# Expert slots numbered by expert and rank, a row gather for every pair of experts, 18 ring slots, and a down projection that leaves its two halves for combine

## The chip, the cores and the metric

The kernel runs on one core of one Trainium2 chip. The metric is the device time of one execution in microseconds; the median of three runs is given, and one more execution was taken with the profiler.

## The reference

Two transformer-like blocks over 256 tokens of width 1024, batch 1, in fp32. The first has a projection, sparse attention, retention and a merge. The second has a state-space branch, latent attention, a cross attention over a memory, and then the mixture of experts that this change is about. All of it up to the router is the same in both kernels. Cut to what matters:

```python
def hierarchical_moe(h, w_rg, b_rg, w_re, b_re, w_gate, w_up, w_down):
...
    g_prob = jax.nn.softmax(g_logits, axis=-1)
    g_sel = jnp.argmax(g_logits, axis=-1)
...
    top_v, top_i = lax.top_k(e_in, TOP_K)
    w_top = jax.nn.softmax(top_v, axis=-1) * g_w
    expert_id = g_sel[:, None] * EXPERTS_PER_GROUP + top_i
    combine = jnp.sum(jax.nn.one_hot(expert_id, N_EXPERTS, dtype=jnp.float32) * w_top[..., None], axis=1).astype(t.dtype)
    hg = jnp.einsum('td,edf->tef', t, w_gate)
    hu = jnp.einsum('td,edf->tef', t, w_up)
    act = jax.nn.silu(hg) * hu * combine[:, :, None]
    y = jnp.einsum('tef,efd->td', act, w_down)
...
h = h + hierarchical_moe(rms_norm_2(h, norm_moe[i]), ...)
...
return rms_norm_2(h, norm_final)
```

A token belongs to one of 4 groups of 8 experts, and goes through two experts of its group: silu(x W_gate) * (x W_up), times W_down (256 x 1024), times a weight; the two results are added to the residual h. The 256 tokens give 512 (token, expert) entries, called slots.

## The kernel before

All dense projections run from a stream of 1 MB weight units: SyncE loads a unit into `raw` (3 slots), ScalarE makes `whi` and POOL `wlo` of it (3 slots each), and TensorE multiplies in three fp32r passes. The last units are those of `xo` (output of the cross attention) and `rt` (the router, unit 111). After them comes the part that changes.

The expert weights (three parts of an expert: gate/up rows 0 to 511, gate/up rows 512 to 1023, down; each 1 MB) are loaded by SyncE (L507 for "e" entries, L515 for "o" entries) into a ring of `NRING` = 13 slots of 8 KB per partition. Experts are worked on in pairs. `pair_plan` gives 24 pairs in a fixed order: 16 pairs "e" of two experts each, and 8 pairs "o" that take what an expert has over `TS` = 32 tokens. The loads of an "o" pair have a condition and are skipped on the chip when there is nothing over; the matmuls of an "o" pair run in any case. Before the first load of an "o" pair SyncE waits for `over_ready` (L510), the table of these further tiles, that VectorE makes in `overflow()`. An entry of the ring waits until the unit that held its slot has been used (`first_used`, `gu_full` or `y_full`). The first four slots lie in memory that is free early, the others only after the router's matmuls (`weights_used` = NU).

Slots are packed: the 512 entries, sorted by expert, stand in 512 columns. VectorE makes `pick` (256 tokens x 512 slots, ones where a token fills a slot), and TensorE gathers all rows at once (L2345, L2346: the normed rows split in two fp32r parts, 8 blocks of 128 features with 512 moving columns), ScalarE copies the result to `xs`. Then, for each pair, POOL cuts the window of 32 columns of each expert out of `xs` (L547, `window`) and the slots' weights out of `wrow` (L554, `weights`).

For each pair j TensorE does: `gate_up(j)` (L2393: 32 fp32 matmuls with 32 stationary columns, in four column groups of the array), `act_transposed` (L2378), `down` (L2409: 8 fp32 matmuls of 512 columns into four column groups of one bank, accumulated over the two halves k of the hidden width), and `combine` (L2419: 4 fp32r matmuls with `sT`, the one-hot map from slots to tokens, into the banks ps4 to ps7 that accumulate over all pairs). In this order: `gate_up(j)` with the transposes of j-1 within it, `combine(j-2)`, `down(j-1)`. ScalarE does `silu` (L903) and `y_hi` (L909, L910), VectorE `gate` (L1695), `act_copy` (L1703, which multiplies with the slots' weights), `owners` (L1711, L1713: makes `sT`) and `y_lo` (L1720: the rest of the split of y in fp32r parts, four instructions on 32 partitions). At the end VectorE adds the residual (L1782), ScalarE squares (L922), VectorE scales (L1790), and four stores go out.

Of the kernel before, what the change touches and what calls it, by code (L numbers as in the profile page):

```python
# [22 lines left out]
UW = 2048  # L23
# [11 lines left out]
NRING = 13  # L35
# [6 lines left out]
for _n, _w in (("ident", 128), ("tri", 128), ("stri", 128), ("ones", 128), ("cmpmask", 30), ("cos", 16), ("sin", 16),  # L42
               ("invf", 16), ("iota", 32), ("rcos", 128), ("rsin", 128), ("negmask", 128), ("slot", 1)):
    CONST[_n] = (sum(w for _, w in CONST.values()), _w)
# [72 lines left out]
def pair_plan():  # L117

    pairs = []
    for n in range(NEXP // 2):
        pairs.append(("e", n))
        if n % 2 == 0 and n or n == 3:
            pairs.append(("o", len(pairs) - n - 1))
    return pairs


def ring_plan(npair):


    ring = []
    for j in range(npair + 1):
        if j < npair:
            ring += [(j, part, u) for part in range(2) for u in range(2)]
        if j:
            ring += [(j - 1, 2, u) for u in range(2)]
    return ring


def bank_plan(units):
# [58 lines left out]
    G += [("xg", k) for k in range(8)]  # L200
# [24 lines left out]
    W += [("rtt", 0), ("cn", 0), ("ds", 0), ("wr", 0), ("pT", 0), ("od", 0)]  # L225
# [12 lines left out]
def program(nc, x_d, mem_d, pos_d, cst_d, sml_d, dec_d, npost_d, nfin_d, w_d, ew_d, out_d):  # L238
# [9 lines left out]
    NT = len(PAIRS)  # L248
    RING = ring_plan(NT)
    ENTRY = {u: n for n, u in enumerate(RING)}  # L250
    ctx = ExitStack()
    with ctx:
# [128 lines left out]
        xnh = at("xnh", A + 8 * KB, [P, TT, DM], f32r)  # L381
        xnl = at("xnl", A + 16 * KB, [P, TT, DM], f32r)
        pick = at("pick", A + 24 * KB, [P, TT, NSLOT], f32r)
        ramp = at("ramp", A + 28 * KB, [P, NSLOT])
        a = A + 30 * KB
        oh = at("oh", a, [P, 2, TT, 32])
        msum = at("msum", a + 512, [P, TT, 32])
        prod = at("prod", a + 768, [P, 2, TT, 32])
        cnt = at("cnt", a + 1280, [32, P])
        offn = at("offn", a + 1792, [P, 2, 32])  # L390
        row = at("row", a + 2048, [P, 8, 32])
        over = at("over", a + 3072, [P, 8, NOVER])
        posf = at("posf", a + 3584, [P, 4])
        start = at("start", a + 3616, [P, NEXP + NOVER], i32)
        mine = at("mine", a + 3840, [P, NPAIR])
        overi = at("overi", a + 4064, [P, 2, NOVER], i32)
        rtl = at("rtl", A + 38 * KB, [P, 8, TT * 36])
        lgt = at("lgt", A + 38 * KB + 2304, [36, S])
        flt = at("flt", A + 42240, [32, P])
        xw = at("xw", A + 42 * KB, [P, 2, 8, 2 * TS])  # L400
        sg = at("sg", A + 46 * KB, [P, 2, 256])

        yhl = at("yhl", A + 8 * KB, [P, 2, 2, 512], f32r)
        ac = at("ac", A + 28 * KB, [2 * TS, 2, 256])
        tally = at("tally", A, [P, 2, NEXP])
        match = at("match", A + 512, [P, NOVER, NEXP])
        mval = at("mval", A + 512 + 2 * KB, [P, NOVER, NEXP])
        vals = at("vals", A + 512 + 4 * KB, [P, 4, NEXP])
        aT = at("aT", A + 22 * KB, [P, 2, 4 * TS])
        nfin = at("nfin", A + 24 * KB, [P, DM])  # L410
        xs = at("xs", base + 9 * UW * 4, [P, 8, NSLOT])
        a = base + 9 * UW * 4 + 16 * KB
        posT = at("posT", a, [P, 2 * S])
        sT = at("sT", a + 2 * KB, [P, 2, S], f32r)
        wrow = at("wrow", a + 4 * KB, [P, NSLOT])
        wx = at("wx", a + 6 * KB, [P, 2, 2 * TS])
        wpick = at("wpick", a + 8 * KB, [P, TT, NSLOT])
        diag = at("diag", a + 12 * KB, [P, 4, P])
        wtmp = at("wtmp", a + 14 * KB, [P, NSLOT])
        ring = [at(f"ring{i}", A + (48 + 8 * i) * KB if i < 4 else base + (i - 4) * UW * 4, [P, UW])[:, :] for i in range(NRING)]  # L420

# [56 lines left out]
        def _(sp):  # L478
# [40 lines left out]
        def _(pool):  # L519
# [14 lines left out]
            nc.gpsimd.iota(ramp[:, :], [[1, NSLOT]], base=0, channel_multiplier=0, allow_small_or_imprecise_dtypes=True).then_inc(sem("ramp_ready"), 1)  # L534

            starts = {}

            def window(j):
                kind, k = PAIRS[j]
                if kind == "o":  # L540
                    pool.wait_ge(sem("over_ready"), 1)
                k = 2 * k + NEXP * (kind == "o")
                starts[j] = [pool.value_load(start[0:1, k + u:k + u + 1], min_val=0, max_val=NSLOT - TS) for u in range(2)]
                if j >= 2:
                    pool.wait_ge(sem("gu_full"), j - 1)
                for u in range(2):
                    ins = pool.tensor_copy(xw[:, j % 2, :, TS * u:TS * u + TS], xs[:, :, bass.ds(starts[j][u], TS)])  # L547
                ins.then_inc(sem("rows_ready"), 1)

            def weights(j):  # L550
                if j >= 2:
                    pool.wait_ge(sem("aT_ready"), j - 1)
                for u, first in enumerate(starts.pop(j)):
# [1978 lines left out]
```

## Time and profile before

| | before |
|---|---|
| median of three runs | 1198.32 us (1196.86 to 1198.56) |
| the profiled execution | 1198.53 us |
| its span, first to last instruction | 1196.7 us |
| PE busy | 1023.9 us (86%) |
| POOL busy | 612.6 us (51%) |
| DVE busy | 619.5 us (52%) |
| ACT busy | 426.6 us (36%) |
| mean granted TensorE clock | 0.931 |
| DMA in the last quarter of the span | up to 421 GB/s |

The span is what the trace shows; the execution's own time has 1.83 us more. PE is TensorE's matmuls, PEld its weight loads, DVE VectorE, ACT ScalarE, SPq the queue of SyncE. Matmuls overlap in the records, so the spacing of their starts says more than their durations. An fp32 matmul is two instructions in the trace, an fp32r one or a transpose is one.

### The profile page before, as it was taken

What the parts mean: (1) busy time and instruction counts of PE and PEld (TensorE: products, weight loads), DVE (VectorE), ACT (ScalarE), POOL (GpSimd) and SP (SyncE); (2) the same over time, 40 slices, a digit from 0 to 9 for tenths busy, and PEclk for the clock granted to TensorE, in tenths of its full rate; (3) what the DMA queues carried; (4) which work ended last, traced back from release to release, by engine and by line L of the source; (5) the groups of instructions that cost most, each with busy time, mean ns of one, the idle gap of its engine ahead of it and who ended that gap; (6) DMA issues with size and microseconds to landing.
All of it is one profiled execution on the core that took longest, in us unless ns stands there. A gap on an engine that the chain in (4) does not pass through costs nothing.

```text
span 1196.7 us, 19506 instructions
## 1 busy us (share of the span) xinstructions
PE 1023.9 (86%) x7452; PEld 840.0 (70%) x7452; DVE 619.5 (52%) x1343; ACT 426.6 (36%) x637; POOL 612.6 (51%) x549
## 2 busy tenths in 40 slices
PE   5897899987957979999999999999985879787773
PEld 4786788987946869999977789898964534333331
DVE  6303246368545665554159986842116656444445
ACT  4543333332224545554434344344432311111111
POOL 5997814456748676664765349888540011110100
PEclk9999898999987889999999999999996879999996
DMA  6554522333334344332433226554434589999990
GB/s 251 172 204 160 192 71 71 100 131 123 140 107 141 139 143 141 139 121 96 145 137 106 97 81 211 176 172 170 155 138 189 234 340 413 420 421 420 420 398 36
DMA packets 31907, 224.90 MB, mean 188 GB/s; under 512 B 3664, under 2 KB 3664, under 8 KB 5072
## 3 DMA queue, kind: packets, MB, share of 16 engines
q1 hardware_dynamic: 30672, 220.07, 48.9%
q10 hardware_dynamic: 1152, 3.67, 0.9%
q8 instruction: 59, 0.97, 0.3%
q14 instruction: 24, 0.20, 0.0%
HBM read 273.01 MB, written 1.05 MB: 229 GB/s over the span
## 4 chain that ended last, share of the span: by engine, by line
POOL 44%; issue 31%; DMA 12%; PE 9%; DVE 3%; SPq 0%; ACT 0%; POOLq 0%; DVEq 0%
POOL wlo L524 44%; DMA ring<-in_experts 12%; PE ps L2393 3%; PE ps L2409 1%; PE ps L2419 1%; DVE yhl L1720 1%; PE ps L2345 0%; PE ps L2346 0%; PE ps L1807 0%; PE ps L1809 0%; PE ps L1808 0%; PE ps L2378 0%; POOLq L527 0%; DVE x L1782 0%; SPq L507 0%
## 5 line engine op out<-in xcount | busy, mean ns | idle before, releaser
L524 POOL TENSOR_TENSOR wlo<-raw,whi 128x512 fp32r<-128x512 f32 x448 | 583.6, 1336 | 308.4 <-ACT whi L580 307.9
L1857 PE MATMUL ps<-xhi,whi 128*128 128x256 f32 x960 | 283.6, 295 | 10.5 <-DVE xlo L1210 4.1
L1858 PE MATMUL ps<-xhi,wlo 128*128 128x256 f32 x960 | 277.7, 289 | 0.0
L1859 PE MATMUL ps<-xlo,whi 128*128 128x256 f32 x960 | 277.4, 289 | 0.0
L580 ACT ACTIVATE whi<-raw 128x2048 fp32r<-128x2048 f32 x112 | 214.0, 1914 | 147.0 <-PE ps L1859 75.2
L1857 PEld LDWEIGHTS ps<-xhi,whi 128*128 128x128 f32 x960 | 191.0, 199 | 14.7 <-issue 7.1
L1858 PEld LDWEIGHTS ps<-xhi,wlo 128*128 128x128 f32 x960 | 190.6, 199 | 1.0 <-issue 0.7
L1859 PEld LDWEIGHTS ps<-xlo,whi 128*128 128x128 f32 x960 | 190.4, 198 | 0.0
L2393 PE MATMUL ps<-ring,xw 128*32 128x256 f32 x1536 | 103.6, 407 | 33.0 <-DMA ring<-in_experts 32.3
L1807 PE MATMUL ps<-whi,xhi 128*128 128x512 f32 (+3 forms) x298 | 117.8, 395 | 13.1 <-POOL wlo L524 11.1
L547 POOL COPY xw<-xs 128x256 f32 x48 | 20.4, 452 | 209.9 <-PE ps L2393 162.7
L1808 PE MATMUL ps<-wlo,xhi 128*128 128x512 f32 (+3 forms) x298 | 114.9, 386 | 0.0
L1809 PE MATMUL ps<-whi,xlo 128*128 128x512 f32 (+3 forms) x298 | 114.6, 385 | 0.0
L2393 PEld LDWEIGHTS ps<-ring,xw 128*32 128x32 f32 x1536 | 52.7, 114 | 77.3 <-issue 58.3
L1720 DVE TENSOR_TENSOR yhl<-ps,yhl 32x512 fp32r<-32x512 f32 x96 | 65.9, 687 | 75.9 <-ACT yhl L910 74.8
L1807 PEld LDWEIGHTS ps<-whi,xhi 128*128 128x128 f32 x298 | 57.6, 193 | 26.6 <-POOL wlo L524 10.5
L1808 PEld LDWEIGHTS ps<-wlo,xhi 128*128 128x128 f32 x298 | 57.6, 193 | 10.7 <-issue 1.0
L1809 PEld LDWEIGHTS ps<-whi,xlo 128*128 128x128 f32 x298 | 57.6, 193 | 10.3
L1150 DVE TENSOR_REDUCE stat<-ps 128x1 f32<-128x128 f32 (+1 forms) x36 | 11.0, 306 | 90.0 <-PE ps L1918 69.7
L2409 PE MATMUL ps<-ring,aT 128*32 128x512 f32 x384 | 49.0, 629 | 9.6 <-issue 6.8
L903 ACT ACTIVATE sg<-ps 128x256 f32<-128x256 f32 x24 | 9.2, 384 | 119.2 <-PE ps L2393 119.2
L658 ACT ACTIVATE pr<-ps,stat 128x128 f32<-128x128 f32 x64 | 26.2, 415 | 55.8 <-DVE stat L1151 55.8
(465 smaller groups left out, 1496.0 us busy)
## 6 DMA issues: line engine op xcount, KB each, us to landing
ring<-in_experts SPq DMA_DIRECT2D x144, 1024.0 KB
raw<-in_weights SPq DMA_DIRECT2D x112, 1024.0 KB, 4.9
x<-in_x SPq DMA_DIRECT2D x2, 512.0 KB, 4.5
memt<-in_mem ACTq DMA_DIRECT2D x1, 1024.0 KB, 6.0
out<-xn ACTq DMA_DIRECT2D x4, 256.0 KB, 2.5
decay<-in_decay ACTq DMA_DIRECT2D x1, 512.0 KB, 4.1
npost<-in_norm_post ACTq DMA_DIRECT2D x1, 512.0 KB, 5.4
nfin<-in_norm_final ACTq DMA_DIRECT2D x1, 512.0 KB, 8.1
```

The costliest lines, as they stand in the source:

```text
L524: ins = pool.tensor_tensor(wlo[:, j, c], raw[:, j, c], whi[:, j, c].bitcast(f32), ALU.subtract)
L580: act.activation(whi[:, n % NSPL, :], raw[:, n % NRAW, :], ACT.Copy).then_inc(hi_ready, 1)
L658: ins = act.activation(p_buf[:, c], pj((S_, u))[:, c], ACT.Exp, bias=stat[:, NMAX + k + t:NMAX + k + t + 1], accum_out=stat[:, sums + k + ...
L1720: ins = v.tensor_tensor(yhl[other, j % 2, b, :], ps[3][own, :], yhl[own, j % 2, b, :].bitcast(f32), ALU.subtract)
L1807: mm(out, lh, rh, start=first, stop=False, skip_group_check=skip)
L1808: mm(out, lh, rl, start=False, stop=False, skip_group_check=skip)
L1809: return mm(out, ll, rh, start=False, stop=last, skip_group_check=skip)
L1857: mm(o_, wh[:, k, cc], hi[:, k0 + r0 + k, :], start=first, stop=False, skip_group_check=True)
L1858: mm(o_, wl[:, k, cc], hi[:, k0 + r0 + k, :], start=False, stop=False, skip_group_check=True)
L1859: ins = mm(o_, wh[:, k, cc], lo[:, k0 + r0 + k, :], start=False, stop=last, skip_group_check=True)
L2393: ins = mm(ps[j % 2][q:q + TS, 0:256], xw[:, j % 2, 4 * part + k, TS * u:TS * u + TS], wt[u][:, k, 256 * h:256 * h + 256], start=first, st ...
L2409: ins = mm(ps[3][q:q + TS, :], aT[:, j % 2, 2 * TS * k + TS * u:2 * TS * k + TS * u + TS], wt[u][:, k, 512 * h:512 * h + 512], start=k == ...
```

## The change

- Slots are numbered by expert and rank: expert e owns slots 32e to 32e + 31, and entries beyond rank 31 get slots of the further tiles. `rank` comes from one product with the mask `before` over `msum`.
- The gather is done for each pair, from the unsplit fp32 `xn`: `gather(j)` on TensorE (16 matmuls with a 128x128 stationary part of `xn` and 64 moving columns of `pick`), then `rows_out` on VectorE writes `xw`. `pick` is made for each pair by `pick_rows` from `codes` (VectorE). The gather of 512 columns, `xs`, `wrow`, `wpick` and POOL's copies go; POOL makes only an iota in this stage.
- The slots' weights come from one more small product (`slot_weights`, `weights_of_slots`) as one column per pair in `wslot`, and are put on in `y_hi` and `y_lo`.
- The ring has 18 slots, in places that come free at three times: four as before; entries 4 to 6 in the `raw` slots, entries 7 to 13 once `weights_used` is NU - 1, entries from 14 on once it is NU. Entries stand in the order of the pairs.
- The "o" pairs stand at other places in the order; the first is the fifth pair (before, the fourth).
- TensorE's order for a pair: `gate_up(j)`, `gather(j+1)`, `act_transposed(j)`, `combine(j-1)`, `down(j)`. With j = 0, `code_rows` and `weights_of_slots` come in between, with j = 1 `residual_in`.
- `down` writes one bank per half h of the output columns, and its column groups hold (expert u, half k of the hidden width); the sum over k happens in `combine`, which takes eight matmuls (h, token tile t, part). The y parts are made in two instructions each, of 128 partitions.
- The residual enters ps4 to ps7 through a product with the identity; the last norm's squares and scaling read these banks.

```diff
-NRING = 13
+NRING = 18
@@ pair_plan
-        if n % 2 == 0 and n or n == 3:
+        if n in (3, 4, 5, 7, 9, 11, 13, 14):
@@ ring_plan
+    return [(j, part, u) for j in range(npair) for part in range(3) for u in range(2)]
@@ SyncE
-                if n == 4:
+                if 4 <= n < 7:
+                    sp.wait_ge(lo_ready, NU - 6 + n)
+                if n == 7:
+                    sp.wait_ge(weights_used, NU - 1)
+                if n == 14:
                     sp.wait_ge(weights_used, NU)
@@ ScalarE
+            def y_hi(j):
                 act.wait_ge(sem("y_full"), j + 1)
+                w = wslot[:, PLACE[j]:PLACE[j] + 1]
+                for h in range(2):
+                    act.activation(yhl[:, h, 0, :], ps[2 + h][:, :], ACT.Copy, scale=w).then_inc(sem("y_hi_ready"), 1)
+            act.wait_ge(sem("combined"), NT)
             for t in range(TT):
+                for h in range(2):
+                    k = STAT["f"] + 2 * t + h
+                    act.activation(xn[:, t, 512 * h:512 * h + 512], ps[4 + 2 * t + h][:, :], ACT.Square, accum_out=stat[:, k:k + 1]).then_inc(sem("squares_f"), 1)
@@ VectorE
+            def pick_rows(j, at_):
+                do(v.tensor_tensor(hit[:, :, :], C("iota").unsqueeze(1).to_broadcast([P, 4, 2 * TS]), ALL4(at_, 2 * TS), ALU.is_equal))
+                sync()
+                v.tensor_tensor(pick[:, j % 2, :, :], hit[:, 0:2, :], hit[:, 2:4, :], ALU.add).then_inc(sem("pick_ready"), 1)
+            def rows_out(j):
+                dve.wait_ge(sem("gathered"), j + 1)
+                v.tensor_tensor(xw[:, j % 2, :, :], ps[1][:, :].rearrange("p (k s) -> p k s", k=8),
+                                D("g_moe").unsqueeze(2).to_broadcast([P, 8, 2 * TS]), ALU.mult).then_inc(sem("rows_ready"), 1)
             def owners(j):
+                do(v.tensor_scalar(own[:, :], posT[:, :], -2.0 * TS * PLACE[j], C("slot"), ALU.add, ALU.is_equal))
+                sync()
+                v.tensor_tensor(sT[:, j % 2, :], own[:, 0:S], own[:, S:2 * S], ALU.add).then_inc(sem("owners_ready"), 1)
             def y_lo(j):
+                for h in range(2):
+                    dve.wait_ge(sem("y_hi_ready"), 2 * j + h + 1)
+                    v.scalar_tensor_tensor(yhl[:, h, 1, :], ps[2 + h][:, :], wslot[:, PLACE[j]:PLACE[j] + 1],
+                                           yhl[:, h, 0, :].bitcast(f32), ALU.mult, ALU.subtract).then_inc(sem("y_lo_ready"), 1)
             for j in range(NT):
                 if j:
                     y_lo(j - 1)
                 gate(j)
+                if j + 1 < NT:
+                    rows_out(j + 1)
                 act_copy(j)
                 if j == 0:
+                    slot_weights()
+                    wait_full(dve, ("ws", 0))
+                    release(v.tensor_copy(wslot[:, :], pj(("ws", 0))[:, 0:NPAIR]), ("ws", 0))
+                    wait_done(dve, ("ws", 0))
+                    further()
+                    wait_done(dve, ("pT", 0))
+                owners(j)
+                if j + 2 < NT:
+                    pick_rows(j + 2, codes[:, PLACE[j + 2], :])
@@ TensorE
+            def gather(j):
+                pe.wait_ge(sem("pick_ready"), j + 1)
+                for k in range(8):
+                    for t in range(TT):
+                        ins = mm(ps[1][:, 2 * TS * k:2 * TS * k + 2 * TS], xn[:, t, k * P:k * P + P], pick[:, j % 2, t, :], start=t == 0, stop=t == 1)
+                ins.then_inc(sem("gathered"), 1)
             def down(j):
+                for h in range(2):
+                    for u in range(2):
+                        for k in range(2):
+                            q = TS * (2 * u + k)
+                            ins = mm(ps[2 + h][q:q + TS, :], aT[:, 2 * TS * k + TS * u:2 * TS * k + TS * u + TS], wt[u][:, k, 512 * h:512 * h + 512], start=True, stop=True)
+            def combine(j):
+                pe.wait_ge(sem("owners_ready"), j + 1)
+                for h in range(2):
+                    pe.wait_ge(sem("y_lo_ready"), 2 * j + h + 1)
+                    for t in range(TT):
+                        for part in range(2):
+                            ins = mm(ps[4 + 2 * t + h][:, :], sT[:, j % 2, t * P:t * P + P], yhl[:, h, part, :], start=False, stop=part == 1 and j == NT - 1)
+            for j in range(NT):
+                gate_up(j)
+                if j == 0:
+                    code_rows()
+                if j + 1 < NT:
+                    gather(j + 1)
+                act_transposed(j)
+                if j == 0:
+                    weights_of_slots()
+                if j == 1:
+                    residual_in()
+                if j:
+                    combine(j - 1)
+                down(j)
             combine(NT - 1)
```

## Rows read from the trace of the kernel before

**Rows 1.** Chain of waits, 860 to 1197 us, shares by line.
```profile
by line: DMA ring<-in_experts 41.6%; PE ps L2393 11.1%; issue 9.0%; PE ps L2409 4.9%; POOL wlo L524 3.7%; PE ps L2419 3.3%; DVE yhl L1720 2.5%; PE ps L2345 1.6%; PE ps L2346 1.4%; PE ps L1807 1.3%; PE ps L1809 1.3%; PE ps L1808 1.3%; PE ps 
```
**Rows 2.** Windows: length, busy us of each engine (instructions), clock, DMA share, GB/s.
```profile
900.00:910.00 10.00, 5.81 (x30) 4.47 (x29) 6.45 (x21) 5.47 (x12) 0.56 (x1) 0.75 0.00 0
...
920.00:930.00 10.00, 6.88 (x23) 5.94 (x23) 6.38 (x27) 0.69 (x1) 0.00 (x0) 0.50 1.01 425
...
950.00:960.00 10.00, 4.19 (x66) 2.05 (x54) 9.40 (x27) 0.97 (x2) 1.04 (x4) 0.81 0.18 75
960.00:970.00 10.00, 9.43 (x90) 3.85 (x86) 5.07 (x11) 1.47 (x3) 1.24 (x4) 0.68 0.73 284
...
1040.00:1060.00 20.00, 16.11 (x164) 7.47 (x168) 7.52 (x15) 2.74 (x6) 2.35 (x8) 0.83 1.01 421
```
**Rows 3.** DMA queues, 860 to 1197 us: packets, MB, share.
```profile
q1 hardware_dynamic: 13972, 101.72, 73.1%
```
**Rows 4.** Waits of SyncE's queue, 860 to 1197 us: total, times, longest.
```profile
SPq L510 <- DVE mine L1661: 12.7, 1, 12.7
```
**Rows 5.** Timeline of TensorE near 1000 us: start, length, line, tiles, count.
```profile
999.15 1.20 PE L2419 MATMUL ps<-yhl,sT 128*128 128x512 f32 x4
1000.33 1.92 PE L2409 MATMUL ps<-ring,aT 128*32 128x512 f32 x16
1002.04 2.80 PE L2393 MATMUL ps<-ring,xw 128*32 128x256 f32 x48
1004.78 0.34 PE L2378 MATMUL ps<-cst,ac 64*128 64x64 f32 x2
```
**Rows 6.** Timeline from the last dense unit to the first pairs.
```profile
899.92 0.40 PE L1809 MATMUL ps<-whi,xlo 128*128 128x512 f32 x1
...
904.95 1.57 PEld L1892 LDWEIGHTS ps<-cst,xn 128*128 128x128 f32 x8 [3.65 <-DVE xn L976]
...
919.08 1.06 PE L2327 MATMUL ps<-cst,msum 128*32 128x128 f32 x4 [5.74 <-DVE msum L1623]
...
923.44 0.29 DVE L1628 TENSOR_TENSOR prod<-oh,ps 128x128 f32<-128x128 f32 x1 [2.98 <-PE ps L2337]
...
936.61 1.88 PE L2352 MATMUL ps<-wpick,cst 128*128 128x512 f32 x4
...
938.32 1.05 PE L2356 MATMUL ps<-diag,cst 128*128 128x128 f32 x8
...
940.59 6.25 PE L2393 MATMUL ps<-ring,xw 128*32 128x256 f32 x112 [0.65 <-ACT posT L598]
...
947.88 0.68 DVE L1744 TENSOR_TENSOR mval<-cst,tally 128x512 f32<-128x512 f32 x1
```
**Rows 7.** Groups by line, 880 to 1197 us: busy, mean ns, idle before.
```profile
L2393 PE MATMUL ps<-ring,xw 128*32 128x256 f32 x1536 | 103.6, 407 | 33.0 <-DMA ring<-in_experts 32.3 <-ACT posT L598 0.7
L1720 DVE TENSOR_TENSOR yhl<-ps,yhl 32x512 fp32r<-32x512 f32 x96 | 65.9, 687 | 75.9 <-ACT yhl L910 74.8
...
L1695 DVE TENSOR_TENSOR ac<-sg,ps 32x256 f32<-32x256 f32 x48 | 20.1, 418 | 25.2 <-ACT sg L903 24.5
...
L909 ACT ACTIVATE yhl<-ps 128x512 fp32r<-128x512 f32 x24 | 14.3, 597 | 84.0 <-PE ps L2409 84.0
```
**Rows 8.** Timeline of TensorE in the scan stage, near 614 us.
```profile
614.00 1.89 PE L2226 MATMUL ps<-xtok,segM 128*128 128x64 f32 x16
615.73 0.65 PE L2209 MATMUL ps<-segR,cst 128*128 128x512 f32 x1
```
**Rows 9.** Timeline of TensorE in a dense projection, near 100 us.
```profile
100.29 0.28 PE L1857 MATMUL ps<-xhi,whi 128*128 128x256 f32 x1
100.41 0.28 PE L1858 MATMUL ps<-xhi,wlo 128*128 128x256 f32 x1
```
**Rows 10.** Timeline of the tail, after the last combine.
```profile
1184.87 2.48 DVE L1782 TENSOR_TENSOR x<-ps,x 128x512 f32<-128x512 f32 x4 [2.23 <-PE ps L2419]
...
1192.33 1.41 DVE L1790 SCALAR_TENSOR_TENSOR xn<-x,stat,nfin 128x512 f32<-128x512 f32 x2
```

More of the change, by code:

```diff
@@ L391, in program @@
[L391 to L420, printed above, removed]
+        a = [A + 8 * KB]
@@ new lines, in program @@
+        msum = small("msum", [P, TT, NEXP])
+        prod = small("prod", [P, 2, TT, NEXP])
+        cnt = small("cnt", [NEXP, P])
+        flt = small("flt", [NEXP, P])
+        tally = small("tally", [P, 2, NEXP])
+        match = at("match", a[0], [P, NOVER, NEXP])
+        mval = at("mval", a[0] + 2 * KB, [P, NOVER, NEXP])
+        nfin = small("nfin", [P, DM])
+        over = small("over", [P, 2, NOVER])
+        overi = small("overi", [P, 2, NOVER], i32)
+        choice = small("choice", [P, 8, 4])
@@ new lines, in program @@
+        posT = small("posT", [P, 2 * S])
+        xw = small("xw", [P, 2, 8, 2 * TS])
+        ac = small("ac", [2 * TS, 256])
+        aT = small("aT", [P, 4 * TS])
+        slots = [A + (48 + 8 * i) * KB for i in range(4)]
+        slots += [base + 8 * KB * i for i in (1, 2, 0)]
+        slots += [base + 8 * KB * i for i in (4, 7, 5, 8)] + [base + 80 * KB, base + 96 * KB, A + 40 * KB]
+        slots += [base + 8 * KB * i for i in (3, 6)] + [base + 72 * KB, base + 88 * KB]
+        ring = [at(f"ring{i}", o, [P, UW])[:, :] for i, o in enumerate(slots)]
@@ L533, in _ @@
             pool.wait_ge(sem("mn_ready"), 2)
[L534 to L553, printed above, removed]
-                    ins = pool.tensor_copy(wx[:, j % 2, TS * u:TS * u + TS], wrow[:, bass.ds(first, TS)])
-                ins.then_inc(sem("wx_ready"), 1)
-            pool.wait_ge(sem("start_ready"), 1)
-            for k in range(4, 8):
-                wait_done(pool, ("xg", k))
-            window(0)
-            window(1)
-            wait_done(pool, ("wr", 0))
-            for j in range(NT):
-                weights(j)
-                if j + 2 < NT:
-                    window(j + 2)
+            nc.gpsimd.iota(islot[:, :], [[TS, 2], [0, 2], [1, TS]], base=0, channel_multiplier=0, allow_small_or_imprecise_dtypes=True).then_inc(sem("islot_ready"), 1)
         @block.scalar
@@ new lines, in _ @@
+            do(v.tensor_scalar(flt[:, :], cnt[:, :], float(TS), None, ALU.is_gt))
+            for q in range(2, NSTEP + 1):
+                sync()
+                ins = v.scalar_tensor_tensor(flt[:, :], cnt[:, :], float(TS * q), flt[:, :], ALU.is_gt, ALU.add)
+                if q < NSTEP:
+                    do(ins)
+            ins.then_inc(sem("more_ready"), 1)
+            rows_out(0)
+            wait_full(dve, ("od", 0))
+            release(v.tensor_copy(tally[:, :, :], pj(("od", 0))[:, 0:64].rearrange("p (a e) -> p a e", a=2)), ("od", 0))
@@ L2362, in _, with code_rows, weights_of_slots @@
             end(ins, ("od", 0))
-            od_bank = JOBS[("od", 0)][0]
-            for b in range(8):
-                if b != od_bank:
-                    pe.wait_ge(bank_done[b], TOTAL[b])
+            def code_rows():
+                pe.wait_ge(sem("diag_ready"), 1)
+                begin(("pT", 0))
+                for i in range(4):
+                    ins = mm(pj(("pT", 0))[:, i * P:i * P + P], ones, diag[:, i, :], start=i == 0, stop=i == 3, skip_group_check=True)
+                end(ins, ("pT", 0))
+            def weights_of_slots():
+                pe.wait_ge(sem("which_ready"), 2)
+                begin(("ws", 0))
+                for i in range(4):
+                    ins = mm(pj(("ws", 0))[:, 0:NPAIR], which_slot[:, i, :], which_pair[:, i, :], start=i == 0, stop=i == 3)
+                end(ins, ("ws", 0))
             def unit(j, part, u):
@@ L2392, in gate_up @@
                                 q = TS * (2 * u + h)
[L2393 to L2395 removed]
+                                ins = mm(ps[0][q:q + TS, 0:256], xw[:, j % 2, 4 * part + k, TS * u:TS * u + TS], wt[u][:, k, 256 * h:256 * h + 256], start=first, stop=last)
                     if part == 0:
```

329 lines of the change are left out of this document (116 added, 213 removed).

## Prediction

> **What bounds the kernel now.** I read the page first, then the chain of waits, the windows, the DMA view and the timeline, all for the last 337 us, because the diff touches only what follows the last dense projection. In that stretch the chain is held by the expert weights: 41.6% is DMA into the ring, against 11.1% for the gate/up matmuls [rows 1]. The windows show why: from 960 to 1160 us the 16 DMA engines stand at a share of 1.01 and about 421 GB/s while TensorE is busy 16 of 20 us [rows 2]. A unit is 1,048,576 bytes, so it takes 1.0486 / 0.421 = 2.49 us. The queue moved 101.72 MB [rows 3], which is 97 units: one raw unit and the 96 of the sixteen "e" pairs. So no expert had more than 32 tokens, the eight "o" pairs load nothing, and TensorE still does their matmuls. DMA lies idle twice: around 900 to 910 us (0 GB/s), and around 950 to 960 us (75 GB/s), where the queue stands 12.7 us at the overflow table [rows 2, 4].
>
> The reader should see that there are two clocks in this stage. DMA needs 96 x 2.49 = 239 us. TensorE needs 24 pairs times what one pair costs it, and now that is less. Start to start in the timeline at full clock: 48 gate/up instructions 2.74 us, four combine instructions 1.18, sixteen down instructions 1.71; the two transposes have 0.33 with their fill, some 0.27 to the next start [rows 5]. All 64 gate/up instructions are thus 2.74 x 64/48 = 3.65 us, and a pair is 3.65 + 0.27 + 1.18 + 1.71 = 6.8 us, 163 us for 24. It ends second.
>
> **The change, part by part.**
>
> *Ring of 18 slots, loads from earlier.* Units 4 to 6 go into raw slots, units 7 to 13 once the last xo unit is used (its last matmul starts at 899.92 [rows 6]), and 14 to 17 after the router. That uses the idle DMA window: 14 x 2.49 = 35 us of loading, of which nine units ran at this place before. All 18 are there by about 928. The other 78 need 78 x 2.49 = 194 us and could end near 1126, where they end near 1165 now. The first overflow pair also comes later in the list (unit 24), and its table needs fewer operations. By itself this part is worth some 30 to 40 us, if DMA stays the bound.
>
> *The gather, new in every pair.* Instead of one gather of 512 columns (32 fp32r instructions) and cheap POOL copies, each pair does 16 fp32 matmuls with a 128x128 stationary part of xn and 64 moving columns. An fp32 matmul is two instructions in this trace (768 gate/up calls are 1536 records [rows 7]), so 32 per pair. The trace has this very form: 16 instructions of 128x64 fp32, each with fresh 128x128 weights, run from 614.00 to the next group at 615.73, 1.73 us or 108 ns each [rows 8]; it has four such groups at full clock, all of 1.73. The gather is 3.46 us. The lower bound is that the weights hide behind the moving side, as for the 256-column fp32r instructions, which start every 120 ns, 13 more than their 107 ns of columns [rows 9]: 64 fp32 columns at the 0.43 us per 512 of four instructions in 1.71 us [rows 6] are 53 ns, 1.7 to 2.1 us in all. The upper bound is the cold 200 ns per weight load [rows 6], 6.4 us. I take 3.46, the row of the same form. The Trainium skill, "TensorE: Matmul & The Clock Gate", section "LDWEIGHTS (loading the stationary operand)", prices a load by columns over 1.2 GHz, 107 ns for 128, and the row agrees (108).
>
> *Down and combine.* Down keeps 8 calls, 16 instructions and four column groups, only with k in the group instead of the accumulation: 1.71 us as before. Combine goes from four instructions to eight. The form (fp32r, 512 columns) has 213 ns of columns plus some 14; four more are 0.91 us: 1.18 + 0.91 = 2.09.
>
> *Sum for one pair:* 3.65 + 3.46 + 0.27 + 2.09 + 1.71 = 11.18 us. The lower bound, 53 ns per gather instruction, is 9.4; a few tenths for hand-overs give 11.8.
>
> *Is it back to back?* VectorE per pair: y_lo 2 x 0.69, gate 2 x 0.42 [rows 7], act_copy 0.29 as another 128x128 from PSUM [rows 6], rows_out and owners at some 0.7 each for 512 columns, pick_rows about 0.65; under 6 us. silu and gate (0.4 + 0.84) lie under the 3.46 of the next gather; rows_out and act_copy (1.0 after the gather) under transposes and combine (2.36); y_hi and y_lo (2.6 after down) under gate/up. So no wait is left inside a pair. POOL leaves the stage, which costs nothing. Loads: the longest run of e, e, o needs 2 x 14.9 = 30 us of DMA against 33.5 of TensorE, so the ring is full when asked. TensorE takes over as the bound.
>
> *Front.* The masks' matmuls start at 919.08 [rows 6]. Then the two ds matmuls (1.0 us cold), prod and reduce 0.29 each, three small ones and pick_rows (together 1.3): gather(0) starts near 922.1. TensorE is at half clock there (0.50, its 1.2 GHz [rows 2]), so 32 x 0.215 = 6.9 us, the cold load and a little; ready 929.0, rows_out 0.8, gate/up(0) at 929.9. It starts at 940.59 now [rows 6], so 10.7 us earlier. The whole hi/lo gather, wpick, wrow and most of the tile table go from this path.
>
> *First two pairs.* Gate/up(0) to 933.5; code_rows 1.0 [rows 6]; gather(1) to 938.0; transposes 938.3. Then TensorE waits for VectorE: rows_out, act_copy and the 13 operations of slot_weights (4.1), so 942.4; ws 1.0, down(0) 945.1, gate/up(1) 948.8. VectorE meanwhile does further() (seven operations, six at 0.69 [rows 6], 4.4), owners and pick_rows(2): gather(2) starts at 949.7, not 948.8. Then 3.46, transposes 0.27, the residual through the identity (8 instructions x 0.43 = 3.44), combine 2.09, down 1.71: 960.7. The 4 us of idle before ws can drop the clock, as an idle TensorE did at 950 to 970 (0.81, then 0.68 [rows 2]). Ten microseconds at 0.68 lose 3.2; I add 2.3, for the idle here is shorter. Pair 1 ends at 963.
>
> *Rest.* 22 pairs x 11.18 less the one gather that the last lacks (3.46) is 242.5: down(23) ends at 1205.5. Behind it two y_hi (0.6 [rows 7] and 0.55), the second y_lo 0.69, half a combine 1.15 and hand-overs: 3.1, so 1208.6. The tail is 11.83 now, 1184.87 to 1196.7 [rows 10]. The four adds (2.48) go; four squares of 512 with accumulator reads replace two of 1024, and the first now waits for both halves. By the chain: 1.4 of squares, 1.9 of root, 1.4 of scaling, 1.9 and 1.4 again, 3.0 of store: 11.0. Span 1219.6.
>
> The profiled execution took 1198.53 us for a span of 1196.7, so 1.83 lie outside; 1221.4. It was 0.21 above the median of 1198.32, so I say 1221.
>
> **The rivals.**
>
> A. *The gather's weight loads hide* (ends on the other side). The place is the 32 instructions of each gather. For it: the 120 ns rows [rows 9]. Against: the groups of the same form show 108 ns [rows 8]. At 57 ns a gather is 1.8 us, 1.65 less in 23 of them, 38 us: 1183. It decides from the point where a gather takes less than 2.45 us (77 ns per instruction): then the 23 us lost are given back. Chance 0.09.
>
> B. *The loads hide in part.* Half way between 57 and 108 ns is 82: 0.83 less in each of 23 gathers, 19 us: 1202. No row of this form shows it. Chance 0.06, half of it within 0.2%. The Trainium skill bears on it: the same page, section "Back-to-back issue gap", gives about 81 ns for a sustained stream of loads and matmuls of 128 columns, and one of the 64-column fp32 instructions streams as long as such a matmul.
>
> C. *DMA stays the bound.* The chain would again show ring loads; the end would be 1126 plus the last pairs and tail, near 1155, or 1160. That needs pairs under 9 us on TensorE, so A and more. Chance 0.02.
>
> D. *Hand-overs or the clock cost more.* If each pair waits 1 us (down on act_copy, or gather on pick_rows), 22 us: 1243. If TensorE ran half of the first 30 us cold besides, 1250. For it: TensorE works through five hand-overs a pair, and I cost them at nothing; against: each of them has over 1 us of cover by the durations above. Chance 0.14.
>
> My forecast itself: 0.69.
>
> **How the numbers follow.** Faster or slower by 0.2% (2.4 us) is what a measurement can tell. Faster: A, C and a tail of B, 0.12. Same: 0.03. Slower: 0.85. The likeliest case has its own range: the pair between 10.7 and 11.7, 22 times, and 4 us either way in the front, 1208 to 1235. The range takes in B and most of D: 1201 to 1241.
>
> **What would show it.** Right: the chain of waits names the gather, gate/up, down and combine lines and hardly DMA; TensorE over 95% busy and its clock at full (2.4 GHz) from 965 on; gather groups of 32 instructions 3.4 to 3.6 us apart from the next group; pairs 11.2 us apart, also the "o" pairs; DMA gaps inside each cycle, last ring load 20 us and more before the last combine; gate/up(0) near 930. Wrong: gather groups near 2 us (A); DMA share still 1.01 after 1000 (C); idle before down, or before the gather, ended by VectorE (D); a last load that comes after TensorE has asked for it.

## The result, and the profile after

| | before | after |
|---|---|---|
| median, us (range) | 1198.44 (1196.86 to 1200.69, 4 runs) | 1224.18 (1223.84 to 1226.33, 4 runs) |
| profiled execution, us | 1198.53 | 1223.84 |
| its span, us | 1196.7 | 1222.1 |
| granted TensorE clock, mean | 0.931 | 0.954 |

After over before is 1.0222, with a 95% interval from 1.0201 to 1.0244. The changed kernel is slower, at a higher mean clock.

The chain that ended last, from 860 us on, answers to [rows 1]; the line gives shares by engine and source line:

```profile
by line: PE ps L2290 25.5%; PE ps L2346 23.5%; PE ps L2376 13.6%; PE ps L2359 12.8%; issue 5.0%; POOL wlo L528 2.4%; PE ps L2333 1.7%; PE ps L1766 1.2%; PE ps L1768 1.2%; PE ps L1767 1.1%; PE ps L2368 1.0%; DVE xn L1749 0.6%; DVE stat L927
```

L2290 is the gather, L2346 gate/up, L2376 combine and L2359 down. DMA into the ring, 41.6% before, is on the chain no more. The windows of after answer to [rows 2] (length, then busy time and instructions of PE, PEld, DVE, ACT and POOL, then the granted clock, DMA share and GB/s):

```profile
920.00:930.00 10.00, 10.00 (x77) 7.84 (x80) 4.06 (x16) 0.00 (x0) 0.00 (x0) 0.55 0.52 214
940.00:950.00 10.00, 10.00 (x96) 5.11 (x96) 7.76 (x16) 1.65 (x3) 0.00 (x0) 0.70 0.52 191
950.00:960.00 10.00, 10.00 (x58) 6.18 (x61) 2.58 (x7) 0.00 (x0) 0.00 (x0) 1.00 0.15 61
1040.00:1060.00 20.00, 20.00 (x223) 14.56 (x216) 8.54 (x19) 3.05 (x6) 0.00 (x0) 1.00 0.89 350
1180.00:1200.00 20.00, 20.00 (x208) 13.85 (x211) 7.57 (x17) 2.91 (x5) 0.00 (x0) 1.00 0.17 70
```

TensorE is busy in all of the 20 us where it was idle 4 before, POOL is gone, and DMA has gaps: 350 GB/s at 1040, 70 at 1180, where the last loads end about 27 us before the last combine does. The timeline of TensorE shows the front, one whole pair and the end (start, duration, then the form, its count, and the idle time before it):

```profile
918.07 7.06 PE L2290 MATMUL ps<-pick,xn 128*128 128x64 f32 x32 [1.06 <-DVE pick L1599]
926.05 5.09 PE L2346 MATMUL ps<-ring,xw 128*32 128x256 f32 x64
...
939.26 1.90 PE L2322 MATMUL ps<-which_pair,which_slot 128*128 128x24 f32 x8 [3.25 <-DVE which_pair L1702]
941.09 3.64 PE L2359 MATMUL ps<-ring,aT 128*32 128x512 f32 x16
944.51 4.40 PE L2346 MATMUL ps<-ring,xw 128*32 128x256 f32 x64
948.84 3.79 PE L2290 MATMUL ps<-pick,xn 128*128 128x64 f32 x32
...
960.05 3.64 PE L2346 MATMUL ps<-ring,xw 128*32 128x256 f32 x64
...
971.41 3.64 PE L2346 MATMUL ps<-ring,xw 128*32 128x256 f32 x64
974.97 3.79 PE L2290 MATMUL ps<-pick,xn 128*128 128x64 f32 x32
978.69 0.34 PE L2333 MATMUL ps<-cst,ac 64*128 64x64 f32 x2
978.95 2.13 PE L2376 MATMUL ps<-yhl,sT 128*128 128x512 f32 x8
981.02 1.92 PE L2359 MATMUL ps<-ring,aT 128*32 128x512 f32 x16
982.76 3.64 PE L2346 MATMUL ps<-ring,xw 128*32 128x256 f32 x64
...
1203.43 0.33 PE L2333 MATMUL ps<-cst,ac 64*128 64x64 f32 x2 [1.39 <-DVE ac L1660]
...
1205.76 1.93 PE L2359 MATMUL ps<-ring,aT 128*32 128x512 f32 x16
1209.37 2.10 PE L2376 MATMUL ps<-yhl,sT 128*128 128x512 f32 x8 [1.68 <-DVE yhl L1676]
```

Read from start to start, a pair is 3.56 gate/up, 3.72 gather (3.71 in most pairs), 0.26 transposes, 2.07 combine and 1.74 down: 982.76 less 971.41 is 11.35 us. No row of it carries an idle time. Down is the old 1.7 us, combine twice the old, and the gather is new.

### The profile page after: what moved, and what is told of

The parts are those of the page before. It is cut to its first block, busy times and chain, and to the rows that moved or that the text cites. A ratio compares the mean times of both kernels' runs of the same rounds, so it can differ in the third digit from the quotient of the medians.

```text
span 1222.1 us, 20669 instructions
## 1 busy us (share of the span) xinstructions
PE 1102.9 (90%) x8286; PEld 930.8 (76%) x8286; DVE 601.9 (49%) x1342; ACT 423.1 (35%) x630; POOL 584.2 (48%) x453
## 4 chain that ended last, share of the span: by engine, by line
POOL 43%; issue 29%; PE 25%; DVE 2%; POOLq 0%; ACT 0%; DVEq 0%
POOL wlo L528 43%; PE ps L2290 8%; PE ps L2346 7%; PE ps L2376 4%; PE ps L2359 4%; PE ps L2333 1%; PE ps L1766 0%; PE ps L1768 0%; PE ps L1767 0%; PE ps L2368 0%; POOLq L531 0%; DVE xn L1749 0%; DVE stat L927 0%; PE ps L2322 0%; PE ps L2269 0%
## 5 line engine op out<-in xcount | busy, mean ns | idle before, releaser
L1766 PE MATMUL ps<-whi,xhi 128*128 128x512 f32 (+3 forms) x298 | 117.4, 394 | 12.6 <-POOL wlo L528 10.6
L2290 PEld LDWEIGHTS ps<-pick,xn 128*128 128x128 f32 x768 | 90.8, 198 | 10.5 <-issue 10.5
L2290 PE MATMUL ps<-pick,xn 128*128 128x64 f32 x768 | 94.0, 283 | 1.1 <-DVE pick L1599 1.1
L872 ACT ACTIVATE yhl<-ps,wslot 128x512 fp32r<-128x512 f32 x48 | 30.3, 683 | 186.0 <-PE ps L2359 186.0
L2346 PE MATMUL ps<-ring,xw 128*32 128x256 f32 x1536 | 89.5, 386 | 0.0
L2346 PEld LDWEIGHTS ps<-ring,xw 128*32 128x32 f32 x1536 | 50.3, 112 | 45.1 <-issue 16.9
L1767 PEld LDWEIGHTS ps<-wlo,xhi 128*128 128x128 f32 x298 | 57.3, 192 | 10.6 <-issue 1.0
L1676 DVE SCALAR_TENSOR_TENSOR yhl<-ps,wslot,yhl 128x512 fp32r<-128x512 f32 x48 | 33.8, 746 | 63.2 <-ACT yhl L872 63.2
L2376 PE MATMUL ps<-yhl,sT 128*128 128x512 f32 x192 | 51.5, 410 | 1.7 <-DVE yhl L1676 1.7
```

What stands on the lines that cost most here:

```text
L1766: mm(out, lh, rh, start=first, stop=False, skip_group_check=skip)
L1767: mm(out, lh, rl, start=False, stop=False, skip_group_check=skip)
L2290: ins = mm(ps[1][:, 2 * TS * k:2 * TS * k + 2 * TS], xn[:, t, k * P:k * P + P], pick[:, j % 2, t, :], start=t == 0, stop=t == 1)
L2346: ins = mm(ps[0][q:q + TS, 0:256], xw[:, j % 2, 4 * part + k, TS * u:TS * u + TS], wt[u][:, k, 256 * h:256 * h + 256], start=first, stop=last)
L2376: ins = mm(ps[4 + 2 * t + h][:, :], sT[:, j % 2, t * P:t * P + P], yhl[:, h, part, :], start=False, stop=part == 1 and j == NT - 1)
```

## The experiments

Each kernel ran beside the kernel before on the same chip; "e" kernels are edits of the changed kernel unless said otherwise. Two things were to be told apart: what a pair's gather costs and why, and what the ring and the early loads are worth.

**Which side of a gather instruction sets its time?** The 32 instructions of a gather take 3.71 us, 116 ns each on average. Here they have half the moving columns and all the weight loads. It leaves the rows of each pair's second expert out.

```diff
-  ins = mm(ps[1][:, 2*TS*k:2*TS*k + 2*TS], xn[...], pick[:, j % 2, t, :], ...)
+  ins = mm(ps[1][:, 2*TS*k:2*TS*k + TS],   xn[...], pick[:, j % 2, t, 0:TS], ...)
```

> The changed kernel with gathers of 32 moving columns instead of 64, still 16 matmuls (32 instructions), each with its own 128x128 weights. The rows of the second expert of each pair are left out. Theory (the weight loads set the spacing of the gather's instructions, 116 ns in the changed kernel): nothing changes, 1224 us within 4, gathers still near 3.7 us. Rival (the streamed columns count, by themselves or added to the load): 32 fp32 columns less are 27 ns per instruction, 0.85 us per gather, 20 us in all: 1204.

Measured: 1252.12 us beside 1199.86, a ratio of 1.0442 (1.0382 to 1.0503). TensorE's timeline:

```profile
1048.51 3.76 PE L2290 MATMUL ps<-pick,xn 128*128 128x32 f32 x32
1052.20 0.34 PE L2333 MATMUL ps<-cst,ac 64*128 64x64 f32 x2
1052.47 3.19 PE L2376 MATMUL ps<-yhl,sT 128*128 128x512 f32 x8
...
1065.33 2.14 PE L2376 MATMUL ps<-yhl,sT 128*128 128x512 f32 x8
...
1076.66 3.44 PE L2376 MATMUL ps<-yhl,sT 128*128 128x512 f32 x8
```

The gather takes 1052.20 less 1048.51, 3.69 us or 115 ns an instruction, as with 64 columns. So the moving side does not set it. That it is the weight load is inferred by exclusion: what was halved did not count, and a load comes with each instruction. Nor is it a price that every instruction has, for the 64 of gate/up start every 56 ns in the same kernel. But the kernel got 28 us slower in the median, and its profiled span 30.2 us longer (1252.3 against 1222.1), with less work. The combine behind this gather took 3.19 us, the next one 2.14, as at full clock, and the one after it 3.44: 12 of the last 21 are slow. Down behind a slow one is in part slow too, so that a pair takes 11.33 us from one quick combine to the next (1065.33 to 1076.66), and 12.86 from a slow one (1052.47 to 1065.33). Twenty pairs up to the last take 243.3 us, 16.3 more than in the changed kernel. Of the rest of the 30.2, 9.0 lie ahead of the change: the masks' matmuls started at 923.95, not 914.96 (see "Left open"). Another 3.4 are lost between the masks and the combine at 980.00, mostly at half clock, and 1.5 from the combine at 1223.28 to the end. The same kernel's windows, over one such combine, the next gather and its combine:

```profile
1040.00:1043.00 3.00, 3.00 (x8) 2.12 (x7) 1.81 (x6) 0.00 (x0) 0.00 (x0) 0.51 1.01 426
...
1048.50:1052.20 3.70, 3.70 (x36) 3.65 (x32) 0.83 (x2) 0.38 (x1) 0.00 (x0) 1.00 1.01 425
1052.50:1055.50 3.00, 3.00 (x9) 1.97 (x8) 2.15 (x6) 0.00 (x0) 0.00 (x0) 0.62 0.80 333
```

The clock is granted in full during the gather and falls to half (1.2 of 2.4 GHz) in the work behind it, though the profile counts TensorE as busy all along. A second width, 48 columns (16 rows of each second expert left out), asks whether this is gradual:

```diff
+  ins = mm(ps[1][:, 2*TS*k:2*TS*k + 48], xn[...], pick[:, j % 2, t, 0:48], ...)
```

> The changed kernel with gathers of 48 moving columns, between the 64 of the change and the 32 of the first experiment; 16 rows of each second expert are left out. Theory (spacing is the weight load's): gathers of 3.7 us as with 32 and 64. For the clock: with 32 columns it fell to half in the combine behind each gather, with 64 it did not. If this goes by what the array streams in a gather, 48 columns fall between: fewer or no stretches at half clock, 1224 to 1250. If the fall with 32 columns was an accident of that run, 48 columns show full clock throughout and 1224.

Measured: 1245.70 beside 1197.78, 1.0405 (1.0365 to 1.0446). The gather again takes 3.70 us. The combines behind it run at full clock or not, in one timeline:

```profile
1042.17 3.77 PE L2290 MATMUL ps<-pick,xn 128*128 128x48 f32 x32
...
1046.14 2.13 PE L2376 MATMUL ps<-yhl,sT 128*128 128x512 f32 x8
...
1057.81 3.27 PE L2376 MATMUL ps<-yhl,sT 128*128 128x512 f32 x8
```

Of the last 21 combines with a gather before them 11 are slow, and twenty pairs take 243.2 us, as with 32 columns. So it is not gradual between these two, as I had thought it might be; with the 64 columns of the changed kernel no combine from 960 us on is slow. The gather's time is the same in all three.

**What is the gather worth as a whole?** Half of its instructions, in every pair, then seven eighths of them from pair 2 on; as many of the rows' features are left out.

```diff
-  for k in range(8):
+  for k in range(4):                   # e2
+  for k in range(8 if j < 2 else 1):   # e3
```

> The changed kernel with 8 of the 16 matmuls of each gather (feature blocks 0 to 3); the other half of the features is left out. Theory (TensorE's own instructions are the bound from end to end): 16 x 116 ns = 1.86 us less in each of 24 gathers, the first at half clock, some 44 us: 1180, pairs 9.5 us. Rival (a wait behind TensorE takes over at once: ring loads or VectorE): 1195 or more, and idle TensorE before gate/up or down.

> The changed kernel with full gathers for the first two pairs only and one feature block of eight (2 matmuls, 4 instructions) for all others; the rest of the rows is left out, stale ones are used. TensorE would need 11.35 - 3.25 = 8.1 us for a pair. Theory (then the ring loads are the bound again, since two e pairs and an o pair are 24 us on TensorE and 30 us of DMA): 1155 to 1168, DMA share near 1.0 from 1000 us on. Rival (TensorE stays the bound, 71 us less): 1152 or below. Second rival (the ring of 18 brings nothing and the end falls back to that of the kernel before): 1190 or more.

Measured: 1184.71 (0.988, 0.9823 to 0.9937) and 1179.26 (0.9835, 0.9791 to 0.9879), both beside 1199.86. Half a gather less gave 39 us against the changed kernel. The timeline of e2 shows that sixteen instructions do not cost half of 3.71 us:

```profile
1046.15 2.00 PE L2290 MATMUL ps<-pick,xn 128*128 128x64 f32 x16
1048.08 0.34 PE L2333 MATMUL ps<-cst,ac 64*128 64x64 f32 x2
```

They take 1.93 us, so sixteen more add 1.78, 111 ns each, and some 0.15 us belongs to the group as a whole. The other three eighths gave only 5 us more. TensorE's timeline of e3 says why:

```profile
1046.18 0.66 PE L2290 MATMUL ps<-pick,xn 128*128 128x64 f32 x4
1047.63 0.34 PE L2333 MATMUL ps<-cst,ac 64*128 64x64 f32 x2 [0.80 <-DVE ac L1660]
```

The gather was the cover for silu and gate. With 0.66 us of it left the transposes wait 0.80 us a pair for VectorE, 19.4 us in 23 waits, and a pair takes 9.10 us, not 8.1. DMA ran at a share of 1.01 from 1040 to 1060 us, but TensorE waited for the ring only once, 1.6 us. I had expected the loads to be the bound here; they were not yet.

**What are the second bank and the eight combine instructions worth?** Down, y_hi, y_lo and combine as before the change; the gather and the ring as after.

```diff
-  for h: for u: for k: mm(ps[2 + h][q...], ..., start=True, stop=True)
+  for k: for u: for h: mm(ps[3][q...], ..., start=k == 0, stop=k == 1)
-  for h: for t: for part in range(2): mm(ps[4+2*t+h], sT, yhl[:, h, part, :])
+  for t: for h: mm(ps[4+2*t+h], sT, yhl[:, h, 0, :])
```

> One part of the change undone: down accumulates over the halves of the hidden width into one bank again, y_hi copies this bank twice, y_lo is four instructions of 32 partitions, combine four matmuls. All else is as changed. Theory (combine's four further instructions are on the bound, at 1.03 us a pair; y_lo's extra time is under gate/up): 24 x 1.03 less some 1.4 for the longer y_lo behind the last pair, so 23 us less: 1201. Rival (the four slower y_lo instructions, 2.8 us, become a wait in each pair): 1212 or more, with TensorE idle before the transposes.

Measured: 1211.73 beside 1199.86, 1.0106 (1.006 to 1.0151), 12 us less than the changed kernel, where 23 were expected. Its timeline of TensorE:

```profile
1043.71 1.20 PE L2379 MATMUL ps<-yhl,sT 128*128 128x512 f32 x4
...
1054.13 1.20 PE L2379 MATMUL ps<-yhl,sT 128*128 128x512 f32 x4
...
1197.01 2.04 PE L2379 MATMUL ps<-yhl,sT 128*128 128x512 f32 x4 [4.55 <-DVE yhl L1679]
```

A pair is 1054.13 less 1043.71, 10.42 us: 0.93 less, 20.5 us over 22 pairs, as expected. Some 8 are given back outside the pairs. The last combine waits 4.55 us where it waits 1.68 in the changed kernel, and runs at half clock (four instructions in 2.04); the last transposes wait 1.88 against 1.39, the last down takes 2.76 against 1.93. That is about 4.2 us net of the end. The other 3.9 lie ahead of the change: the masks' matmuls started at 918.84 us in this kernel's profile and at 914.96 in the changed one's.

**Is the ring's size worth anything?** Thirteen slots instead of 18, with the rest as after.

```diff
-NRING = 18
+NRING = 13
```

> The changed kernel with a ring of 13 slots instead of 18, loads issued by the same rules. Theory (TensorE is the bound at 11.35 us a pair, and 96 loads take 239 us): the ring's size matters little, within 4 us of 1224, and no pair waits for a ring load over 1 us. Rival (the deeper ring is what keeps the loads ahead, for two e pairs in a row need 30 us of loads): 1232 or more, with TensorE idle before gate/up until a ring load.

Measured: 1228.09 beside 1195.19, 1.027 (1.0221 to 1.032). Pairs are 11.35 us apart, and these are all the waits of TensorE from 950 us on (in all, times, longest):

```profile
PE ps L2376 <- DVE yhl L1676: 1.7, 1, 1.7
PE ps L2333 <- DVE ac L1660: 1.4, 1, 1.4
```

None is for the ring. Five slots more save no wait here. The two profiled spans differ by 3.1 us (1225.2 and 1222.1), of which 2.9 lie ahead of the change (masks at 917.85, not 914.96); the medians differ by 3.9.

**One gather for two pairs.** If an instruction costs 116 ns whatever it streams, 128 columns should cost little more than 64. Rows of two pairs are gathered together, half of the features beside each pair, so that the gate keeps a cover. It leaves nothing out.

```diff
-  for k in range(8): ... mm(ps[1][64 columns of k], xn, pick[64 columns])
+  for k in range(4*(i%2), 4*(i%2) + 4): ... mm(ps[1][128 columns of k % 4], xn, pick[128 columns of two pairs])
```

> The changed kernel with one gather for two pairs: the feature blocks 0 to 3 of both pairs (128 moving columns) beside the first, blocks 4 to 7 beside the second, so each pair has 16 gather instructions instead of 32. Nothing is left out. Theory (weight loads set the spacing, 128 fp32 columns stream in 107 ns and cost about 124 ns per instruction): gathers of 2.0 us instead of 3.71, pairs of 9.65 us, 22 x 1.7 = 37 us less: 1187, give or take 5 for the front. Rival (the columns add to the load: 200 ns and more per instruction): 1215 or more.

Measured: 1184.48 (1179.95 to 1187.9) beside 1195.19, 0.9896 (0.9857 to 0.9936). TensorE's timeline:

```profile
1048.14 2.05 PE L2300 MATMUL ps<-pick,xn 128*128 128x128 f32 x16
1050.12 0.34 PE L2344 MATMUL ps<-cst,ac 64*128 64x64 f32 x2
...
1057.76 2.05 PE L2300 MATMUL ps<-pick,xn 128*128 128x128 f32 x16
```

Sixteen instructions with 128 columns take 1.98 us; e2's sixteen with 64 took 1.93, so twice the columns add 0.05 us to the whole group. A pair takes 9.62 us, 1.73 less than after. From the combine in the third pair's turn to the one in the last pair's, the changed kernel takes 236.1 us (967.60 to 1203.69) and this one 200.9 (963.84 to 1164.76): 35.2 less. The front from the masks on is 7.1 shorter and the masks came 3.3 later, which makes the 39.0 by which the two profiled spans differ (1222.1 less 1183.1). This is the clearest test of the theory: the same rows are gathered, with half the loads, and the loss of the change is gone.

The single records of the traces say what is left. Inside a gather the starts of the instructions are 112 ns apart, with 32, 48, 64 and 128 moving columns alike. The columns show in one place: from the first start to the second it is 132, 147, 160 and 213 ns. After the last start it is 206 ns to the next group in all four. The averages of 115 to 124 ns differ by these two steps and by the length of the group, not by the spacing.

**Both edits, then the ring again.** e7 is e6 with the edit of e4, and e8 is e7 with `NRING` = 13; e9 is e7 with the loads from the fifth on held back until the router. With TensorE at 8.7 us a pair the loads should bind, and the ring and its early loads should count.

```diff
-  if 4 <= n < 7:  sp.wait_ge(lo_ready, NU - 6 + n)      # e9 = e7 with this
-  if n == 7:      sp.wait_ge(weights_used, NU - 1)
-  if n == 14:     sp.wait_ge(weights_used, NU)
+  if n == 4:      sp.wait_ge(weights_used, NU)
```

> The one-bank down and combine of four matmuls together with the gather for two pairs, 18 slots. Nothing is left out. Theory: TensorE needs 8.7 us a pair, 55 us less than the changed kernel over 22 pairs, less 4 for the longer end; two e pairs and an o pair are 26 us of TensorE and 30 of DMA, so ring loads are the bound in part and DMA's share is 1.0: 1165 to 1178. Rival (VectorE's four slow y_lo instructions delay gate and so the transposes now that their cover is 2 us shorter): pairs of 9.5 us and more, idle before the transposes, 1183 or more.

> The same as the two-pair gather with one-bank down, but 13 ring slots. Theory (with TensorE at 8.7 us a pair the loads matter, and the deeper ring carries the o pairs' free time over to the e pairs): 5 to 20 us slower than with 18 slots, TensorE idle before gate/up until ring loads. Rival (the ring's depth is worth nothing even here): within 2 us of it.

> The same kernel as the one with two-pair gathers and a one-bank down, run again beside the next two: within 5 us of its first time, 1174 to 1184.

> The kernel with two-pair gathers, one-bank down and 18 slots, but all entries from the fifth on wait for the router's matmuls, as in the kernel before; only the order in time of 10 loads changes. Theory (the early loads only move idle DMA time: with them the ring stands full and idle until gate/up(0) frees slots, without them the same window is used later): 0 to 5 us slower than the run beside it. Rival (each load started earlier ends the stage earlier, 10 x 2.49 us): 20 us slower or more.

| kernel | median us (range) | before beside it | ratio (interval) |
|---|---|---|---|
| e7 | 1178.74 (1174.03 to 1183.54) | 1195.19 | 0.9873 (0.9825 to 0.9922) |
| e7, again | 1180.35 (1173.56 to 1181.97) | 1197.78 | 0.9862 (0.9834 to 0.9889) |
| e8, 13 slots | 1186.57 (1181.35 to 1187.0) | 1195.19 | 0.9912 (0.9882 to 0.9941) |
| e9, late loads | 1179.49 (1175.53 to 1181.04) | 1197.78 | 0.9847 (0.9818 to 0.9877) |

Pairs of e7 are 8.68 us apart where nothing waits, 0.94 less than e6, yet it gained 6 us in the median and 11 in the profiled span (1172.1 against 1183.1), not 20. The waits of e7, and then the one on the ring in e8, show DMA coming back:

```profile
PE ps L2361 <- DMA ring<-in_experts: 6.0, 3, 3.0
...
PE ps L2390 <- DVE yhl L1687: 4.6, 1, 4.6
...
PE ps L2348 <- DVE ac L1669: 3.8, 2, 1.9
```

```profile
PE ps L2361 <- DMA ring<-in_experts: 11.0, 6, 3.0
```

Against e6 that is 6.0 us for the ring, 2.9 more before the last combine and 1.0 more before transposes, 9.9 in all. That is what is missing in the profiled span.

Here the ring's depth has a price: 8 us between the medians of 18 slots and 13 (1178.74 and 1186.57). The executions of one kernel spread by up to 9.5 us, so the size is rough, but the second series of e7 (1173.56 to 1181.97) lies below nearly all of e8 as well. The two profiled spans differ by 12.5 us (1172.1 and 1184.6). Both kernels reach the combine in the third pair's turn together (961.35 and 960.91 us). Behind it 5.0 us are further waits for the ring, and most of the rest is work at half clock behind such a wait. Half a gate/up behind a wait of the same length, in e7 and then in e8:

```profile
1111.49 1.93 PE L2361 MATMUL ps<-ring,xw 128*32 128x256 f32 x32 [3.04 <-DMA ring<-in_experts]
```

```profile
1088.48 3.32 PE L2361 MATMUL ps<-ring,xw 128*32 128x256 f32 x32 [3.03 <-DMA ring<-in_experts]
```

The early start of the loads has no price that shows (1179.49 without it, 1180.35 with it). With e9 the queue begins some 30 us later and catches up while the first pairs still wait on other things; the same window of e7's second run, then of e9:

```profile
940.00:960.00 20.00, 18.81 (x196) 11.13 (x188) 13.63 (x29) 2.69 (x6) 0.00 (x0) 1.00 0.48 187
```

```profile
940.00:960.00 20.00, 18.80 (x158) 10.05 (x162) 12.05 (x25) 2.69 (x5) 0.00 (x0) 0.86 1.01 421
```

In e7 the ring is full by then and DMA half idle; in e9 DMA does that work there. e7 and e9 are the best of all and cannot be told apart: 1.3 to 1.5% under the kernel before, 3.6 to 3.7% under the changed one.

## Why the prediction came out

It said 1221 and the median is 1224.18, by the mechanism that it named. Step by step:

- **The bound moves to TensorE.** Right, and shown. The gather's cost was tested from several sides: fewer instructions (e2), or the same rows with half the instructions (e6), gave back 39 and 40 us.
- **The pair.** 11.35 against 11.18. The gather was under-sized: 3.71 for 3.46. I read [rows 8] as instructions 108 ns apart. That is an average over a group of 16, and in its single records the starts are 112 ns apart, as in the gather here. Only the first step differs, 55 ns there and 160 here, and the last, 111 there and 206 here. A group of 32 behind gate/up has both dear steps, and the longer spacing 30 times. Gate/up was 0.08 too dear, the rest within 0.03. Over 22 pairs the miss is 3.7 us.
- **Rivals A and B**, that the loads hide, are refuted by the 3.71 us a gather. e1, e10 and e6 show why: with 32, 48, 64 and 128 moving columns the spacing stays, so it is the streaming that hides behind the loads, and not the loads behind it. The Trainium skill, "TensorE: Matmul & The Clock Gate", section "LDWEIGHTS (loading the stationary operand)", gives 107 ns for this load by columns over 1.2 GHz; the traces show starts 112 ns apart in [rows 8] and in every gather, so the rule is near, and some 4% low. The figure of some 81 ns in its section "Back-to-back issue gap", on which rival B leaned, is not reached by any fp32 gather here, the one with 128 columns included.
- **No wait inside a pair.** Right. What I missed is the last pair: it has no gather, and the gather was the cover of silu and gate. Its transposes wait 1.39 us. I had named that cover, and did not ask where it ends; e3 shows the same thing at 0.80 us in every pair.
- **The front.** From the masks' matmuls to the end of pair 1 45.1 us against 43.9. Gather(0) came 3.1 us after them (3.0 predicted), its 7.06 us was 6.9. Gate/up(0) was costed at full clock and ran half cold, 5.09 for 3.65; the wait for the slot table was 3.25 for 4.1; ws and down(0) ran at half clock, 1.90 and 3.64 by their durations, and gate/up(1) took 4.40. I allowed 2.3 us for the clock there. Gather(2) did not wait. But the masks began at 914.96, 4.1 us ahead of [rows 6]. That the change brings this is not shown: six of the eleven profiles of its edits reached them between 917 and 919 us.
- **The end.** From down to the last combine's end 3.8 for 3.1, then 10.6 for 11.0.
- **The sum:** 4.1 less at the start, 1.2 more in the front, 3.7 in the pairs, 1.4 at the last transposes, 0.7 and less 0.4 at the end: 2.5 us more than 1219.6, which is the measured span of 1222.1. An error of −4 and one of +6.5 partly cancelled; that the median was closer than the terms is luck.
- **Rivals C and D.** C did not come: DMA has gaps and TensorE none. In D each half has its trace elsewhere (hand-overs in e3, the clock in e1) but not in the changed kernel behind its first two pairs. One sum in C's ground is off by itself: 928 and 194 us are 1122, not 1126. The forecast did not use it.
- **"By itself this part is worth some 30 to 40 us, if DMA stays the bound"** is not borne out. It was not settled by that part alone, for the old gather was never run with the new ring. But where the loads do bind again at the end (e7 to e9), five slots are worth some 8 us and the early loads 0 within the intervals. The early loads only move idle time of the queue: a full ring then waits for TensorE. By 960 us e9 had moved only two units less than the second e7 since 880 us (19.6 and 21.6 MB), and its stage had begun 4.5 us later (masks at 918.71, not 914.17), the time of two units. All of it together, the deeper ring, the earlier loads, the new order and a wait at the overflow table of under 1 us instead of 12.7, let the last load end at 1145.8 us in e7 and at 1167.4 in the kernel before: 22 us earlier. What the part would be worth by itself stays open, for in e7 the queue stands at a full ring for part of the first pairs.

Of my expectations three missed by much. I took e1 for a kernel as quick as the changed one, e3 for one bound by DMA, and e4 for a full 23 us. In each I had changed one term of the sum and held the others still. e7 ended just over its range (1178.74 and 1180.35 for at most 1178), and e10 landed in its range without the fewer slow stretches that were to bring it there.

**Left open.** The part ahead of the change, the same in all of them, reached the masks' matmuls between 914.17 and 923.95 us over the profiles of the changed kernel and its edits. Without e1 and e10, the two latest, they lie between 914.17 and 918.84. I have not found why. Nearly 5 us of any comparison between two profiles may be this, and 9 where e1 is one of them. Why about every second combine is slow in e1 and e10, and not each, is open too.

## What to carry to other kernels

Where a matmul brings fresh 128x128 fp32 weights and streams few columns, count instructions and not columns: give each load more columns (here two pairs at once, 1.98 us for what took 3.71) before asking for anything else. A prefetch is worth what the compute beside it lets it be: once TensorE took 11.35 us a pair, five more slots saved no wait; with pairs of 8.7 us they were worth some 8 us, and 30 us of earlier loading nothing. Before work is taken off an engine, ask what it was the cover for, in the steady state and in the last turn, where there is no next turn to hide behind.

## What the runs showed of the hardware that I had not expected

The granted clock fell to half behind 12 of 21 gathers that streamed 32 columns an instruction, and behind 11 of 21 with 48, while the profile counts TensorE as 100% busy; with 64 columns at the same spacing it stayed at 1.00 from 950 us to the last pairs. It cost 16 us over twenty pairs, at 32 columns as at 48. A busy share of 100% does not mean that the clock holds: the combine's 2.13 or 3.0 to 3.7 us is where it is seen. Nor do short idle times bring it about by themselves: in e3, with four gather instructions and 0.80 us of idle a pair, the combine kept its 2.1 us.

The starts of fp32 instructions with a fresh 128x128 load were 112 ns apart at 32, 48, 64 and 128 columns. A whole group took more for each than that, by its first and last steps: 115 ns with 32 columns and 116 with 64 in groups of 32, 121 with 64 and 124 with 128 in groups of 16.
